# One decoder step on one core: small early loads sent later or from another queue, one group of bias products behind the rank sums, and every refill of an expert weight slot as two halves

## The reference

```
def decoder_layer(h, mem_k, mem_v, mconv_buf, sconv_buf, ssm_state, lw, prompt):
    a, new_mbuf, new_sbuf, s_new = mixer_block(rmsnorm(h, lw['norm_mix']), ...)
    h = h + a
    h = h + cross_attn(rmsnorm(h, lw['norm_xattn']), mem_k, mem_v, lw['w_xq'], lw['w_xo'])
    h = h + moe(rmsnorm(h, lw['norm_moe']), lw)
...
def expert_ffn(xb, w_gu, b_gu, w_dn, b_dn):
    gu = xb @ w_gu + b_gu                      # 1024 -> 2048
    gate, up = jnp.split(gu, 2, axis=-1)
    gate = jnp.minimum(gate, SWIGLU_LIMIT)
    up = jnp.clip(up, -SWIGLU_LIMIT, SWIGLU_LIMIT)
    glu = gate * jax.nn.sigmoid(SWIGLU_ALPHA * gate)
    return ((up + 1.0) * glu) @ w_dn + b_dn    # 1024 -> 1024
```

## Time and profile before

| what | value |
|---|---|
| time, median of 3 runs | 1408.16 us (1404.67 to 1408.79) |
| time of the profiled execution | 1407.23 us |
| its span, first to last instruction | 1405.5 us |
| PE busy | 1377.9 us, 98% of the span |
| DMA, mean over the span | 354 GB/s |
| the expert pairs | 484.9 us to the end |

### The profile page before, as it was taken

One profiled execution on the slowest core, in us unless ns is written; L12 is line 12 of the kernel. 1 busy time (PEld: TensorE's weight loads), 2 busy tenths in 40 slices (PEclk: granted clock), 3 DMA queues, 4 the chain that ended last, 5 costly groups with the idle time before them and its releaser, 6 DMA issues.

```text
span 1405.5 us, 16097 instructions
## 1 busy us (share of the span) xinstructions
PE 1377.9 (98%) x6416; PEld 668.4 (48%) x6416; DVE 441.4 (31%) x905; ACT 218.3 (16%) x404; POOL 33.7 (2%) x60
## 2 busy tenths in 40 slices
PE   9999999999999999999999999999999999999997
PEld 7688887677756633333333333333333333333332
DVE  5534344962461412221221212212122122221223
ACT  2221022051123311101001011011110111101002
POOL 0000002200002000000000000000000000000000
PEclk9999999999999999999999999999999999999999
DMA  7644545975379899999999999999999999999995
GB/s 249 203 161 154 184 143 190 370 267 206 120 275 389 362 430 389 428 428 428 429 429 428 429 428 429 428 429 428 429 429 428 429 428 428 429 428 429 428 429 208
DMA packets 72120, 497.26 MB, mean 354 GB/s; under 512 B 8968, under 2 KB 10664, under 8 KB 47368
## 3 DMA queue, kind: packets, MB, share of 16 engines
q1 hardware_dynamic: 65852, 478.99, 83.0%
q0 software_dynamic: 4816, 15.54, 3.1%
q10 hardware_dynamic: 1412, 2.18, 0.5%
HBM read 488.61 MB, written 8.24 MB: 354 GB/s over the span
## 4 chain that ended last, share of the span: by engine, by line
PE 94%; SPq 2%; DVE 1%; ACT 1%; DMA 1%; issue 1%; DVEq 0%
PE bank L1504 90%; PE bank L1515 4%; DMA wdt<-in_w_in 1%; DVE wide L1427 1%; SPq L438 1%; ACT wide L615 1%; SPq L441 0%; DVE wide L1487 0%; ACT wide L624 0%; PE bank L1980 0%; ACT L634 0%; ACT L664 0%; SPq L480 0%; SPq L428 0%; DVE wide L1478 0%
## 5 line engine op out<-in xcount | busy, mean ns | idle before, releaser
L1504 PE MATMUL bank<-ring,wide 128*64 128x512 f32 (+2 forms) x1696 | 403.7, 595 | 3.6 <-ACT wide L615 3.0
L1504 PE MATMUL bank<-wide 128*64 128x512 f32 (+6 forms) x1046 | 287.1, 571 | 7.8 <-DVE wide L1427 6.3
L1504 PE MATMUL bank<-tokT,ring 128*128 128x264 f32 x1152 | 264.2, 387 | 0.5 <-DMA ring<-in_w_in 0.5
L1504 PEld LDWEIGHTS bank<-ring,wide 128*64 128x64 f32 (+2 forms) x1696 | 132.6, 140 | 256.1 <-issue 254.7
L1504 PEld LDWEIGHTS bank<-tokT,ring 128*128 128x128 f32 x1152 | 216.7, 190 | 41.9 <-issue 5.6
L1504 PEld LDWEIGHTS bank<-wide 128*64 128x64 f32 (+4 forms) x1046 | 97.9, 152 | 179.9 <-issue 136.4
L1451 DVE TENSOR_SCALAR wide<-bank 128x512 f32<-128x512 f32 x32 | 22.1, 692 | 266.8 <-PE bank L1504 266.8
L615 ACT ACTIVATE wide<-bank 64x512 f32<-64x512 f32 (+2 forms) x103 | 56.0, 559 | 268.8 <-PE bank L1515 216.8
L1504 PE MATMUL bank<-flat,wide 128*64 128x512 f32 (+2 forms) x408 | 92.9, 592 | 2.5 <-ACT wide L615 2.5
L1504 PE MATMUL bank<-conv,wide 128*64 128x512 f32 (+1 forms) x400 | 90.7, 594 | 0.0
L884 ACT ACTIVATE wide<-wide 128x512 f32<-128x512 f32 x32 | 20.2, 631 | 445.2 <-DVE wide L1451 445.2
(11 more groups left out here) (259 smaller groups left out, 721.3 us busy)
## 6 DMA issues: line engine op xcount, KB each, us to landing
ring<-in_w_gate_up SPq DMA_DIRECT2D x64, 2048.0 KB, 21.0
ring<-in_w_down SPq DMA_DIRECT2D x32, 2048.0 KB, 19.5
flat<-in_w_gate_up SPq DMA_DIRECT2D x16, 2048.0 KB, 20.1
conv<-in_w_gate_up SPq DMA_DIRECT2D x16, 2048.0 KB, 20.4
wide<-in_w_gate_up SPq DMA_DIRECT2D x16, 2048.0 KB, 23.8
tokT<-in_w_gate_up SPq DMA_DIRECT2D x16, 2048.0 KB, 21.0
ring<-in_w_in SPq DMA_DIRECT2D x15, 2048.0 KB, 12.2
wide<-in_w_down SPq DMA_DIRECT2D x8, 2048.0 KB, 18.2
```

The source lines that it names most:

```text
L1504: last[0] = pe.matmul(out, lhsT, rhs, start=start, stop=stop)
```

## The change

- `early`: `wdt`, `dtb` and `alog` leave SP's list; ACT issues them (small ones first) after it has emptied the eighth `xT` bank. `dsk` goes from `i == 3` to 6, `gmoe` and `bgu` from 4 to 8, `brt` and `wrt` to 10, `gfin` to 12.
- `turn_x`: for the first four blocks the turns of tiles 2 and 0 come first, before the wait for tile 1, and those of tile 1 after it.
- The second expert's `hidden_bias` goes from ahead of the rank sums to behind them; the `stay_warm` ahead of them shrinks from 512 to 256 columns, and the one behind them goes.
- Each refill becomes two transfers of 1 MB into the same slot. The first waits for `half_done`, a new semaphore that PE raises when a stage has read the first half of its rows, the second for `stage_done`. PE waits for both at the start of the stage (counts of 32 a fill in place of 16), except for chunk 191 as before.

```diff
             def early(i):
-                if i == 3:
-                    sp.dma_start(wdt[:], ...).then_inc(wdt_in, 16)
-                    sp.dma_start(dtb[:], a["dt_bias"].rearrange("l h -> h l")).then_inc(small_in, 16)
-                    sp.dma_start(alog[:], a["a_log"].rearrange("l h -> h l")).then_inc(small_in, 16)
...
-            def refill(g, pair):
+            def refill(g, pair, stages, last=False):
                 i, j = RING[(g - AHEAD) % 8], g % 12
-                sp.dma_start(chunk_view(i, j), moe_chunk(pair, j)).then_inc(moe_full[i], 16)
-            for g, done_stages in zip(range(AHEAD, AHEAD + 8), (1, 2, 3, 5, 6, 7, 8, 9)):
-                sp.wait_ge(S["stage_done"], done_stages)
-                refill(g, g // 12)
+                rows = 1 if j < 8 else 2
+                dst, src = chunk_view(i, j), moe_chunk(pair, j)
+                sp.wait_ge(S["half_done"], stages)
+                sp.dma_start(dst[:, 0:rows], src[:, 0:rows]).then_inc(moe_full[i], 16)
+                sp.wait_ge(S["stage_done"], stages)
+                sp.dma_start(dst[:, rows:2 * rows], src[:, rows:2 * rows]).then_inc(last_half if last else moe_full[i], 16)
+            for g, stages in zip(range(AHEAD, AHEAD + 8), (1, 2, 3, 5, 6, 7, 8, 9)):
+                refill(g, g // 12, stages)
...
         def _(s):
             for k in range(8):
                 move("xT", k, hT[:, k, :], T)
+            s.dma_start(dtb[:], a["dt_bias"].rearrange("l h -> h l")).then_inc(small_in, 16)
+            s.dma_start(alog[:], a["a_log"].rearrange("l h -> h l")).then_inc(small_in, 16)
+            s.dma_start(wdt[:], ...).then_inc(wdt_in, 16)
             move("par0", 0, par[:, 0, :], P)
...
-            stay_warm(bank[7], 512)
-            emptied(pe, "xtok", 3)
-            hidden_bias(first_pair, 0, (1,))
+            stay_warm(bank[7], 256)
             pe.wait_ge(S["mask_ready"], 1)
             b = free_bank(pe, "rank")
...
             close("rank")
-            stay_warm(bank[7], 512)
+            emptied(pe, "xtok", 3)
+            hidden_bias(first_pair, 0, (1,))
             emptied(pe, "xtok", 5)
...
                 def gate_up(e, part):
                     w = landed(4 * e + part)
                     for m in range(2):
...
+                        if m == 0:
+                            last[0].then_inc(S["half_done"], 1)
                     last[0].then_inc(S["stage_done"], 1)
```

More of the change, by code:

```diff
@@ L444, in early @@
                     sp.dma_start(sstate, a["state_short_conv"][0].rearrange("b k (c f) -> (b k) c f", f=256)).then_inc(conv_in, 16)
+                if i == 6:
                     for y in range(2):
@@ L448, in early @@
                                      allow_slow_non_contiguous=True).then_inc(S["dsk_in"], 16)
[L449 removed]
+                if i == 8:
                     sp.dma_start(gmoe[:], a["norm_moe"][0].rearrange("(s p m) -> p s m", p=P, m=2)).then_inc(S["bias_in"], 16)
@@ L453, in early @@
                             .then_inc(S["bias_in"], 16)
+                if i == 10:
                     sp.dma_start(brt[:], a["b_router"][0].partition_broadcast(P)).then_inc(S["bias_in"], 16)
                     sp.dma_start(wrt[:], a["w_router"][0].rearrange("(k p) n -> p k n", p=P)).then_inc(S["bias_in"], 16)
+                if i == 12:
                     sp.dma_start(gfin[:], a["norm_final"].partition_broadcast(P)).then_inc(S["gfin_in"], 16)
@@ L514, in _ @@
                 for g in range(18, 42):
-                    sp.wait_ge(S["stage_done"], it * 24 + (g - 7))
-                    refill(g, (it * 2 + g // 12) % PAIRS)
+                    refill(g, (it * 2 + g // 12) % PAIRS, it * 24 + (g - 7))
             for g in range(12 * PAIRS - 6, 12 * PAIRS):
[L518 to L523, removed]
+                refill(g, PAIRS - 1, n * (12 * PAIRS) + (g - 7), g == 12 * PAIRS - 1)
             sp.wait_ge(S["y_ready"], 1)
@@ L642, in _ @@
                 move("xT", k, hT[:, k, :], T)
+            s.dma_start(dtb[:], a["dt_bias"].rearrange("l h -> h l")).then_inc(small_in, 16)
+            s.dma_start(alog[:], a["a_log"].rearrange("l h -> h l")).then_inc(small_in, 16)
+            s.dma_start(wdt[:], a["w_in"][0].rearrange("(k p) n -> p k n", p=P)[:, :, 3072:3088]).then_inc(wdt_in, 16)
             move("par0", 0, par[:, 0, :], P)
@@ L1524, in _, with turn_x @@
             close("gain")
-            for t in (2, 0, 1):
-                pe.wait_ge(x_in[t], 16)
[L1527 to L1535, removed]
+            def turn_x(ks, tiles):
+                for k in ks:
+                    b = free_bank(pe, "xT", k) if 1 not in tiles or k >= 4 else bank[BANK[JOB["xT", k]]]
+                    for t in tiles:
+                        c, n = TILES[t]
+                        turn(b[:, c:c + n], xtokin[0:n, t, k * P:k * P + P])
+                    if 1 in tiles:
+                        close("xT", k)
+            for t in (2, 0):
+                pe.wait_ge(x_in[t], 16)
+            turn_x(range(4), (2, 0))
+            pe.wait_ge(x_in[1], 16)
+            turn_x(range(4), (1,))
             b = free_bank(pe, "rbc")
@@ L1540, in _ @@
             close("rbc")
-            turn_x(range(4, KB))
+            turn_x(range(4, KB), (2, 0, 1))
             pe.wait_ge(par0_in, 16 * 6)
@@ L2096, in landed @@
                     i = RING[(g - AHEAD) % 8] if g >= AHEAD else FIRST_SLOT[j]
-                    fill = 16 * ((g - AHEAD) // 8 + 2)
+                    fill = 32 * ((g - AHEAD) // 8 + 1) + (0 if final and j == 11 else 16)
                     if g < AHEAD:
@@ L2100, in landed @@
                     elif final:
-                        pe.wait_ge(moe_full[i], n * (24 * 16) + fill)
+                        pe.wait_ge(moe_full[i], n * (24 * 32) + fill)
                     else:
-                        pe.wait_ge(moe_full[i], fill if it is None else it * 48 + fill)
+                        pe.wait_ge(moe_full[i], fill if it is None else it * 96 + fill)
                     return [acc[:, 0], acc[:, 1], acc[:, 2], ytok] if i == 9 else [chunk_view(i, j)[:, m] for m in range(2 if j < 8 else 4)]
@@ L2134, in down @@
                                    w[m][:, q * CW:q * CW + CW], False, part == 1 and m == 3)
+                            if m == 1 and q == 1:
+                                last[0].then_inc(S["half_done"], 1)
                         last[0].then_inc(S["stage_done"], 1)
```

3 lines of the change are left out of this document (1 added, 2 removed).

## The result

The changed kernel took 1414.94 us in the median of 8 executions (1411.93 to 1418.12), the kernel before in the same rounds 1407.95 us (8 executions). The ratio is 1.0052, with a 95% interval of 1.0042 to 1.0063: slower by 5.9 to 8.9 us, above the 0.3% that counted as a difference, and above the range of 1402 to 1413. It came out as rival C.

A forecast was written before the change was run, and what follows sets the result against it. PE bounded the kernel, with DMA close behind. 1405.5 less 4.4 (start) and 1.3 (router) is 1399.8; plus 5.8 (refill waits), 0.6 (clock) and 1.7 (execution beyond span) gives 1408 us, range 1402 to 1413.

The forecast's parts named there:

- rival C: Refills: 8 KB rows cost what the 421 GB/s row says or more; slower by over 0.3%, above 1412.4 us; chance 0.16.
- Bound and margin: Expert stages: PE sets the pace and never waits for a chunk; DMA has 1.3 us to spare at chunk 185.
- The cost of 8 KB rows: Expert refills: a 2.097 MB chunk takes 4.95 us in 8 KB rows instead of 4.895; PE waits 5.8 us in all.
- S = 160 x (p - 4.895) - 3.0: PE's total wait for refills over 160 chunks: p is the new time per chunk, 3.0 us the spare; 5.8 us.
- The lead: Refills: the first half issued half a stage sooner starts the stream 1.7 us sooner, raising spare at chunk 185 to 3.0.
- Where the waits stand: Expert stages: one or two a pair from about pair 12, up to about 1.6 us each, the last at stage 185.
- Clock after the last wait: Stage 185: a wait of some 1.5 us may lower PE's granted clock; 0.6 us added.
- The start: Behind the memory turns: issuing `wdt` sooner removes a 2.67 us wait and 1.7 us of slower clock, 4.4 us.
- Rival B: Start: `wdt` on ACT's queue delays first weights and memory tokens; 1410 us expected, 1412.4 at worst; chance 0.07.
- The router: Router: ranks wait for the mask alone and begin sooner, so the gather and all behind it come 1.3 us sooner.
- A: Refills: halves are nearly free, below 4.93 us a chunk; PE's gain stays, 1401.5 up to 1403.9 us; chance 0.22.
- That the change doesn't do what it says: Refills: an issue isn't earlier, so the 1.7 us of lead are missing and the time is 1409.7 us.

The follow-up runs named there:

- e3: The changed kernel with the whole refills of before, issued at the stage's end, keeping the start and router edits; 1402.86 us, ratio 0.9971.
- e6: The kernel before with each refill still one 2 MB transfer but made of 8 KB pieces (wrong weights, only time read); 1416.56 us, ratio 1.0066.
- e2: The kernel before with the split refills alone, first half issued early, start and router as before; 1417.48 us, ratio 1.0086.
- e4: The kernel before with split refills alone, both halves issued at the stage's end; 1418.94 us, ratio 1.0087.
- e5: The kernel before with each refill cut by partitions (0 to 63, 64 to 127), 16 KB rows, both transfers at the stage's end; 2244.65 us.
- e14: The kernel before with each refill cut into even and odd partitions, 16 KB pieces, both transfers at the stage's end; 1407.61 us, ratio 1.0006.
- e11: The kernel before with the router's part alone (second expert's bias products behind the ranks); 1404.31 us, ratio 0.9985.
- e10: The kernel before with each refill still one 2 MB transfer but made of 4 KB pieces (wrong weights, only time read); 1441.10 us, ratio 1.0249.
- e9: The kernel before with the split turns of the prompt and the router's part, small transfers unmoved, whole refills; 1404.42 us, ratio 0.9979.
- e8: The kernel before with the moved small transfers and the router's part, turns in the old order, whole refills; 1402.96 us, ratio 0.9971.
- e12: The kernel before with the moved small transfers and split turns, router as before, whole refills; 1405.61 us, ratio 0.9987.
- e7: The changed kernel with split refills in every other slot only, whole refills in the others; 1408.56 us, ratio 1.0005.
- e13: The changed kernel with split refills for the first eight refills only, whole refills from there; 1403.41 us, ratio 0.9976.
- e15: The changed kernel with whole refills, plus eight unread products of ones in PE's waits in the first 10 us; 1403.08 us, ratio 0.9973.

## Why the prediction was wrong, step by step

**Bound and margin: right.** PE set the pace, with 1.3 us to spare at chunk 185; e3 has the same (landed 1353.06, stage 185 began 1354.38).

**The cost of 8 KB rows: the step that failed.** The form S = 160 x (p - 4.895) - 3.0 was right (e6, without a lead, is 12.3 us later by 0.077 us a chunk, which is 160 chunks), the size of p was not. I had 4.98 from the rate row and 4.90 from the landings of one chunk, and took 4.95. It is 4.972. The rate row was right within 0.01, the landing row misled: it rests on two numbers rounded to tenths, at the end of the queue, and 0.05 us of error in them counts 160-fold. The difference of 0.022 us is 3.5 us of time. Alone it makes 1411.5, still inside the range; with the 1.1 us of the lead and the 2.6 of the start, both below, the sum leaves it. That I leaned to the milder side, and gave what the rate row said a chance of 0.16, is the error; p = 4.972 is inside the forecast's band of 4.93 to 4.978, whose upper end counted the lead and the start in full.

**The lead: over-rated.** I took 1.7 us whole. By the table the halves with lead gain 1.5 (e2) and 0.6 us (after) on those without (e4), one trace each; why after has less than e2 stays open. It adds 1.1 us here. S by the trace of after is 12.1 - 1.3 = 10.8 us, which the ten waits (8.7 and some 2 around them) confirm. With the right p and a lead of 0.6 the formula gives 12.3 - 1.9 = 10.4.

**Where the waits stand: right.** None before about 1100 us, one or two a pair, the last at stage 185. Under 1.6 us each.

**Clock after the last wait: not there.** The granted clock is 1.00 in 1300 to 1400 us of after, and in the 5 us around and behind the wait at 1367.74 (1365 to 1370, 1370 to 1375), so the 0.6 us come off:

```profile
1300.00:1400.00 100.00, 95.00 (x428) 31.44 (x426) 22.11 (x34) 9.42 (x16) 0.00 (x0) 1.00 0.96 401
```

**The start: the second step that failed.** "I take the 4.4 us whole": 2.67 for the wait and 1.7 for the clock. The wait did go, but both numbers were one execution's. Eight traces beside e5 keep the load of `wdt` where it was: waits of 2.67 (before), 2.10 (e2), 2.34 (e4), 2.13 (e6), 2.35 (e14), 1.78 (e11), 0.59 (e10) and 0.17 us (e9). In the last two the lower clock lay in the first projection (19.75 and 19.22 us instead of 18.07), ahead of the wait. There it was free, because the load sets when the products with `wdt` begin: 37.05 to 38.54 us in all eight. That is what I missed. The wait hid PE's slow stretches, and with it gone they count: in after, e3, e8 and e12 the first projection took 20.06, 19.73, 18.89 and 18.99 us. A point behind all this, the four products with `rtok` (51.92 in the trace of before, 51.20 in after), is reached at 50.5 us in the mean of the eight, and at 49.3 in the mean of the six traces with the moved transfers (after, e3, e7, e8, e12, e13; e15, which adds products there, is left out): 1.2 us. The two groups overlap (48.8 to 51.9 and 46.8 to 51.2), so this difference is weak evidence by itself. By time the start is worth 1.8 (e12), which is 2.6 less than I took.

Rival B (the first loads arrive later) isn't seen. Its sign, a wait of PE at about 27 or 30 us, is in none of the six traces. There are waits ahead of the first projection: 2.15 us in after, 1.6 in e7, 0.9 in e12, 0.8 in e3, 0.65 in e8 and 0.5 in e13. But the kernel before has 1.17 us there, the 0.54 of the earlier trace rows and these two (timeline of PE):

```profile
6.16 2.13 PE L1515 MATMUL bank<-ident,flat 128*128 128x128 f32 x12 [0.40 <-DMA flat<-in_x_prompt]
...
11.57 0.33 PE L1515 MATMUL bank<-ident,flat 128*128 128x128 f32 x1 [0.23 <-DMA flat<-in_norm_xattn]
```

and the others that keep the load have 0 to 1.8. Nor can the moved load have made them: in after the last of these waits ended at 10.23 us, and ACT issued `wdt` at 15.88 (in e3 it was 11.96 and 12.56):

```profile
15.88 1.20 ACTq L642 DMA_DIRECT2D wdt<-in_w_in  x1
```

The wait for `rtok` (L957) is only in kernels with the split turns, 0.17 to 1.37 us in five of seven traces: it comes with them and not with the moved loads.

**The router: right.** 1.3 us in the traces of after, e3 and e11. By time 2.1, with 1.3 inside its interval. In the profiled execution of e8 next to nothing of it is left: the granted clock was 0.83 in 470 to 480 us, where it was 1.00 before, and the gather, at 476.57, was 1.82 us sooner with 1.77 of that from the start.

**The sum again.** 1408.0 + 3.5 (p) + 1.1 (lead) + 0.4 (rest of S) - 0.6 (clock) + 2.6 (start) - 0.8 (router) = 1414.2, against 1414.94 measured. The terms were read off after the fact, and those of start and router have intervals of 3 us, so that it closes within 1 us is partly luck.

**Rivals.** A was wrong by its price: 8 KB rows cost 1.6% more (4.972 for 4.895 us), not the 0.6% of its estimate, and not nothing, as the landing row had it. C was right in its mechanism; its condition, p of at least 4.978, was worked out with a start that gained 4.4 us and a lead of 1.7, and with less of both it is met at 4.972. "That the change doesn't do what it says" held in part, as little of the lead survives.

**The better kernel** is the change without its largest part: e3, 1402.86 us, ratio 0.9971 (0.996 to 0.9981) to the kernel before, and 11.3 to 12.1 us below the changed one.

## What to carry to other kernels

Where a DMA stream is the second bound, and by 1 us only, count what an edit does to its time per chunk, times all chunks of the stream: 0.077 us on 2 MB, 1.6%, became 12 us. An earlier issue gained 0.6 to 1.5 us against it, once and not for each chunk. When two rows of a trace disagree on a size that is multiplied by 160, believe the one that rests on more packets, or take the whole spread as the risk; and ask of a wait that is taken away what it had hidden: other delays ahead of it count from then on.

## What the runs showed of the hardware

- A piece has a fixed cost. 2.097 MB took 4.895, 4.972 and 5.12 us in pieces of 16, 8 and 4 KB, with the DMA queue never empty. With the pieces spread evenly over the 16 engines that is 611.9, 310.8 and 160.0 ns a piece, a straight line of about 9.5 ns and 37.6 ns a KB. The number of transfers (1 or 2) made no difference at either length.
- Transfers of 1 MB that write partitions 0 to 63 or 64 to 127 moved 215 GB/s with all engines busy; even and odd partitions, 428.
- SP's issue of a transfer took 0.33 us with six transfers of 128 pieces waiting, but 2 us and up to 5.1 with ten or eleven, 1.5 to 6.5 with six or seven of 256 pieces (e6, 1275 to 1345 us), and in e10, with 512 pieces:

```profile
1312.25 4.71 SPq L509 DMA_DIRECT2D flat<-in_w_gate_up  x1
1317.21 4.71 SPq L509 DMA_DIRECT2D conv<-in_w_gate_up  x1
```

  It looks like a limit on pieces under way. No single count of pieces fits these kernels, so what the limit counts stays open. It is not a limit on transfers: e14 had about thirteen under way, of 64 pieces, and its issues took 0.47 us. The long issues cost nothing that shows here, since the queue was never empty; that an engine with other work than issues would lose the time was not run.
- The granted clock falls for some microseconds in some executions and not in others, and in different places: 10 to 20 us (0.66 in after), 40 to 45 us (0.80 before), 460 to 470 us (0.87 in e15), 470 to 480 us (0.83 in e8 and e12). Inside such a stretch it is 0.50 (12 to 13 us in after, 39 to 42 us before), the lower of the two levels, 1.2 GHz. A wait needn't bring it: behind 2.35 us for `wdt` in e14 the products took 3.73 us, behind 2.10 in e2 5.42. Executions of the kernel before had mean clocks from 0.994 to 0.999, and times from 1402.99 to 1409.08 us (27 of them beside e6). By a straight line through the 27, an estimate, the 0.005 of clock go with 4.5 us of the 6.
